# Keys and probabilities of a latent-attention branch turned by DMA instead of by TensorE

## What is computed

```python
q = (_rmsnorm(q_lat, q_norm_g) @ wq_b).reshape(b, s, MLA_HEADS, MLA_NOPE + MLA_ROPE)
kv = (_rmsnorm(kv_lat, kv_norm_g) @ wkv_b).reshape(b, s, MLA_HEADS, MLA_NOPE + MLA_V)
k_nope, v = kv[..., :MLA_NOPE], kv[..., MLA_NOPE:]
k = jnp.concatenate([k_nope, jnp.broadcast_to(k_pe[:, :, None, :], ...)], axis=-1)
q, k = _rmsnorm(q, qn_g), _rmsnorm(k, kn_g)          # then the last 64 columns are rotated
def attend(q_blk):
    sc = jnp.einsum('bhqd,bhkd->bhqk', q_blk, k).astype(jnp.float32) * scale
    p = jax.nn.softmax(sc, axis=-1)
    return jnp.einsum('bhqk,bhkd->bhqd', p, v)
return jax.nn.silu(gate) * o
```

## Time and profile before

| | |
|---|---|
| runs | 787.21, 787.49, 788.39 us (median 787.49) |
| profiled execution | 787.33 us, of which the trace spans 785.4 |
| TensorE matmuls | busy 779.3 us, 99% of the span |
| DVE / ACT / POOL | busy 558.1 / 417.6 / 65.5 us |
| DMA | 163 MB, 208 GB/s in the mean |
| granted TensorE clock | 1.0 in the mean |

### The profile page before, as it was taken

The page is one execution under the profiler, slowest core; times in us unless marked ns, Lnnn a source line. Parts: engine busy times, 40 slices in busy tenths (PEclk is TensorE's granted clock), DMA queues, the critical chain, the costliest instruction groups (busy, mean ns, idle before and its releaser), DMA issues.

```text
span 785.4 us, 9964 instructions
## 1 busy us (share of the span) xinstructions
PE 779.3 (99%) x3852; PEld 659.7 (84%) x3852; DVE 558.1 (71%) x698; ACT 417.6 (53%) x579; POOL 65.5 (8%) x46
## 2 busy tenths in 40 slices
PE   8999999999999999999999999999999999999998
PEld 7988888888887888888889888888888878888887
DVE  6864599778577756767896727986786597566684
ACT  7576765645344634533564676574545254454331
POOL 0122020100002100000000301100010021000000
PEclk9999999999999999999999999999999999999999
DMA  9796875587562837878766958675674647468785
GB/s 304 275 293 215 240 241 173 174 212 213 176 197 97 261 108 213 229 204 254 223 191 238 280 169 270 195 193 177 152 254 141 184 153 232 136 191 240 203 236 164
DMA packets 97086, 163.02 MB, mean 208 GB/s; under 512 B 57856, under 2 KB 60416, under 8 KB 96912
## 3 DMA queue, kind: packets, MB, share of 16 engines
q1 hardware_dynamic: 96432, 159.93, 67.8%
q10 hardware_dynamic: 432, 1.22, 0.5%
q0 software_dynamic: 176, 1.25, 0.4%
HBM read 147.17 MB, written 2.10 MB: 190 GB/s over the span
## 4 chain that ended last, share of the span: by engine, by line
PE 94%; DVE 3%; ACT 1%; DMA 1%; issue 0%; SPq 0%; ACTq 0%
PE pair L525 65%; PE bank L484 14%; PE pair L484 6%; PE bank L452 1%; PE bank L567 1%; PE bank L445 1%; PE bank L768 1%; PE bank L662 1%; DVE work L1480 1%; DVE lo L1097 1%; PE bank L758 1%; DMA raw<-stream 1%; DVE gate L1398 1%; PE bank L688 1%; PE bank L449 0%
## 5 line engine op out<-in xcount | busy, mean ns | idle before, releaser
L1097 DVE TENSOR_TENSOR lo<-raw,hi 128x1024 fp32r<-128x1024 f32 (+3 forms) x264 | 313.4, 1204 | 125.1 <-ACT hi L805 123.2
L805 ACT ACTIVATE hi<-raw 128x1024 fp32r<-128x1024 f32 (+3 forms) x264 | 264.9, 1021 | 226.0 <-PE pair L525 87.5
L525 PE MATMUL pair<-hi,xT_hi 128*128 128x512 f32 (+1 forms) x768 | 206.0, 388 | 0.7 <-ACT hi L874 0.6
L525 PE MATMUL pair<-lo,xT_hi 128*128 128x512 f32 (+1 forms) x768 | 202.9, 384 | 1.3 <-DVE lo L1097 1.2
L525 PE MATMUL pair<-hi,xT_lo 128*128 128x512 f32 (+1 forms) x768 | 202.8, 384 | 0.0
L525 PEld LDWEIGHTS pair<-lo,xT_hi 128*128 128x128 f32 x768 | 142.6, 188 | 30.3 <-DVE lo L1097 3.0
L525 PEld LDWEIGHTS pair<-hi,xT_lo 128*128 128x128 f32 x768 | 143.2, 188 | 28.1
L525 PEld LDWEIGHTS pair<-hi,xT_hi 128*128 128x128 f32 x768 | 140.7, 188 | 27.7 <-issue 1.1
L484 PE MATMUL bank<-hi,yT 128*128 128x512 f32 x320 | 79.0, 389 | 0.0
L484 PEld LDWEIGHTS bank<-hi,yT 128*128 128x128 f32 x320 | 60.1, 188 | 12.5
L484 PE MATMUL bank<-lo,yT 128*128 128x512 f32 x160 | 42.8, 389 | 0.0
(11 more groups left out here) (176 smaller groups left out, 664.6 us busy)
## 6 DMA issues: line engine op xcount, KB each, us to landing
raw<-stream SPq DMA_DIRECT2D x264, 512.0 KB, 4.3
raw<-stream SPq DMA_DIRECT2D x16, 256.0 KB, 5.1
xT<-x_in SPq DMA_DIRECT2D x16, 128.0 KB, 4.6
out<-xT SPq DMA_DIRECT2D x3, 512.0 KB, 6.7
consts<-consts_in POOLq DMA_DIRECT2D x1, 1152.0 KB, 8.3
mats<-mats_in ACTq DMA_DIRECT2D x2, 576.0 KB, 5.5
turned<-work SPq DMA_TRANSPOSE x34, 4.9
out<-xT SPq DMA_DIRECT2D x4, 128.0 KB, 1.7
```

The lines of the kernel that those rows point to most:

```text
L525: return nc.tensor.matmul(pair[a][m][:, 0:width], x_part[:, slots[i], m * P:(m + 1) * P], w_part[r][:, i * 512:i * 512 + width], start=(sl ...
L805: nc.scalar.activation(cut[0], cut[1], ACT.Copy).then_inc(rounded[r].sem, 1)
L1097: nc.vector.tensor_tensor(cut[0], cut[1], cut[2].bitcast(F32), ALU.subtract).then_inc(split[r].sem, 1)
```

## The change

- Keys (`k`) and probabilities (`p0` for the first 128 queries, `p1` for the others) go by DMA. TensorE's 8 turns of keys and 16 of probabilities per layer go, with the copies out of PSUM behind them.
- u is parted by ACT right behind its making, and its two DMAs stand ahead of granules 45 and 46. The DMAs of k stand ahead of 48 and 49, of p0 ahead of 57 and 58, of p1 ahead of 60 and 61; zb and D move two granules back.
- ACT parts u and k and joins k, D and B; DVE parts p0 and p1 and joins zq, u, p0, p1 and rq. POOL joins nothing.
- `times_v` runs per 128 queries, after granules 58 and 61. ACT's step on the second mixer's output moves from behind granule 83 to behind 85. The rotary key's arithmetic on DVE moves a few instructions back.

```diff
-TURNS = (("zq", 1), ("q", 2), ("u", 1), ("zb", 1), ("D", 1), ("rq", 1), ("B", 1), ("A", 1), ("C", 1),
+TURNS = (("zq", 1), ("q", 2), ("u", 1), ("k", 2), ("p0", 1), ("p1", 1), ("zb", 1), ("D", 1), ("rq", 1), ("B", 1), ("A", 1), ("C", 1),
...
+                if name in ("p0", "p1"):
+                    sp.dma_start_transpose(turned_tile[:, m], halves[:, m]).then_inc(turned.sem, 16)
...
-                    for name, at, parts in (("zq", 20, parts_q), ("q", 39, parts_h), ("u", 55, parts_h),
-                                            ("zb", 64, parts_h), ("D", 68, parts_y), ("rq", 85, parts_r),
+                    for name, at, parts in (("zq", 20, parts_q), ("q", 39, parts_h), ("u", 45, parts_h),
+                                            ("k", 48, parts_k), ("p0", 57, probs_parts[0]),
+                                            ("p1", 60, probs_parts[1]), ("zb", 66, parts_h), ("D", 70, parts_y), ("rq", 85, parts_r),
...
-                for f in range(2):
-                    pe.wait_ge(*la_ready.at(l, f + 1))
-                    pe.wait_ge(*k_scaled.at(l, 1))
-                    turn(2 + f, [kv_sb[:, m, h, 0:NOPE] for h in (2 * f, 2 * f + 1)
-                                 for m in range(MT)]).then_inc(tk_filled.sem, 1)
...
-                turn_probs(0)
-                turn_probs(1)
-                granules(56)
+                granules(59)
+                pe.wait_ge(*probs_ready.at(l, 8))
+                pe.wait_ge(*whole_ready.at(l, TURN["p0"]))
                 times_v(0)
+                granules(62)
+                pe.wait_ge(*whole_ready.at(l, TURN["p1"]))
                 times_v(1)
...
                 take("pv", lambda m: u[:, m, :], x_rs, u_ready)
+                nc.scalar.activation(parts_h, area(6400, 1024).bitcast(U16).rearrange("p (m c a) -> p m a c", m=MT, a=2),
+                                     ACT.Copy).then_inc(parted.sem, 1)
...
+                splits(46)
+                act.wait_ge(*k_scaled.at(l, 1))
+                for m in range(MT):
+                    nc.scalar.activation(parts_k[:, m].rearrange("p a (h c) -> p a h c", h=HEADS),
+                                         kv_sb[:, m, :, 0:NOPE].bitcast(U16).rearrange("p h (c a) -> p a h c", a=2),
+                                         ACT.Copy).then_inc(parted.sem, 1)
...
+                splits(51)
+                join(whole_k, "k")
...
-                splits(84)
+                splits(86)
                 act.wait_ge(*ob_filled.at(l, 1))
...
+                splits(20)
+                join(whole_q, "zq")
...
+                    if d:
+                        join(whole_u, "u")
                     dve.wait_ge(*la_ready.at(l, d + 1))
...
+                splits(56)
+                part_probs(0)
+                splits(57)
+                part_probs(1)
...
                 splits(59)
-                keep_probsT(2)
-                keep_probsT(3)
+                join(probsT[0].rearrange("p h j t -> p (h j t)"), "p0")
...
-                join(whole_u, "u")
-                pool.wait_ge(*k_b_ready.at(l, 2))
-                join(whole_d, "D")
```

More of the change, by code:

```diff
@@ L849, in round_whole, with join @@
                                              ).then_inc(rounded_.sem, 1)
+                def join(words, name):
+                    act.wait_ge(*turned.at(l, 32 * TURN[name]))
+                    nc.scalar.activation(words.bitcast(U16).rearrange("p (t a) -> p a t", a=2),
+                                         turned16[:].rearrange("p (a k) t -> p a (k t)", a=2), ACT.Copy
+                                         ).then_inc(whole_ready.sem, 1)
                 def round_tile(kt):
@@ L980, in _ @@
                                              ).then_inc(kr_rounded.sem, 1)
+                splits(51)
+                join(whole_k, "k")
+                act.wait_ge(*whole_ready.at(l, TURN["k"]))
+                nc.scalar.activation(yT_hi[:, SLOT["A"]:SLOT["A"] + HEADS, :],
+                                     whole_k.rearrange("p (h t) -> p h t", h=HEADS), ACT.Copy,
+                                     scale=gains[:, G_QK + 1:G_QK + 2]).then_inc(kT_rounded.sem, 1)
                 splits(55)
@@ L1054, in _ @@
                 splits(97)
+                join(whole_b, "B")
                 round_whole(whole_b, "B", yTB_rounded, SLOT["B"], G_Y + SLOT["B"])
@@ L1304, in _ @@
                     op0=ALU.mult, op1=ALU.subtract).then_inc(qT_ready.sem, 1)
-                def lo_pair(rounded_, ready, b0, slot0, gain):
-                    for f in range(2):
-                        dve.wait_ge(*rounded_.at(l, f + 1))
-                        at = slice(slot0 + 2 * f, slot0 + 2 * f + 2)
-                        nc.vector.scalar_tensor_tensor(
-                            out=yT_lo[:, at, :], in0=bank[b0 + f][:].rearrange("p (h t) -> p h t", h=2),
-                            scalar=gains[:, gain:gain + 1],
-                            in1=yT_hi[:, at, :].bitcast(F32),
-                            op0=ALU.mult, op1=ALU.subtract).then_inc(ready.sem, 1)
+                zpe = zlat[:, :, LAT_W - ROPE:LAT_W]
+                chained(nc.vector.tensor_tensor(kpe[:], zpe, rope_tab[:, 1, 0], ALU.mult))
+                for a in range(2):
+                    chained(nc.vector.tensor_tensor(kpe_x[:, :, a * half:(a + 1) * half],
+                                                    zpe[:, :, (1 - a) * half:(2 - a) * half],
+                                                    rope_tab[:, 1, 1, :, a * half:(a + 1) * half], ALU.mult))
+                chained(nc.vector.tensor_tensor(kpe[:], kpe[:], kpe_x[:], ALU.add))
                 splits(45)
@@ L1400, in gated @@
                             in1=y[:, m, at], op0=ALU.mult, op1=ALU.mult).then_inc(ready.sem, 1)
-                for m in range(MT):
-                    gated(m, gate0, m, p_inv, yD_ready)
+                splits(61)
+                dve.wait_ge(*gate0_ready.at(l, MT))
+                dve.wait_ge(*pv_done.at(l, 1))
+                gated(0, gate0, 0, p_inv, yD_ready)
+                splits(62)
+                join(probsT[1].rearrange("p h j t -> p (h j t)"), "p1")
+                splits(64)
+                dve.wait_ge(*pv_done.at(l, 2))
+                gated(1, gate0, 1, p_inv, yD_ready)
                 part(gate0_row, yD_ready, 8, parts_y)
@@ L1429, in _ @@
                 splits(68)
+                join(whole_z, "zb")
                 edge = const("edge").rearrange("p (e g t) -> p e g t", e=2, g=4)
@@ L1538, in _ @@
                 splits(89)
+                join(whole_r, "rq")
+                splits(90)
                 part(gate0_row, yB_ready, 8, parts_y)
```

136 lines of the change are left out of this document (49 added, 87 removed).

## The result

| | before | after |
|---|---|---|
| runs, median (us) | 787.49 (787.21 to 788.39) | 807.27 (806.36 to 807.54) |
| ratio, with its 95% interval | 1 | 1.0249 (1.0232 to 1.0266) |
| profiled execution / its span (us) | 787.33 / 785.4 | 806.36 / 804.5 |

Forecast were 799.0 us and 791.5 to 806.5. The direction and the places were right; the price was 19.8 us instead of 11.7.

A forecast was written before the change was run, and what follows sets the result against it. TensorE's matmuls, filling 99% of the span, were taken as the bound. Per layer, waits of 9.6 us less 2.5 removed and 1.2 at granules 85 to 87 gave +5.85; two layers, +11.7 on 787.3: 799.0 us, range 791.5 to 806.5.

The forecast's parts named there:

- another case: Rival: TensorE's clock falls to half rate in its waits, once per layer, giving 804.5 us; chance 12%.

The follow-up runs named there:

- the filled run: The changed kernel with 11 idle matmuls of 512 columns on TensorE between granule 50 and the wait of the scores; measured 804.25 us.

## What to carry to other kernels

A queue that waits for a chain of other engines' work delays every transfer listed behind it: ask of each new entry when its condition comes true, and put it behind the loads that are wanted before that time. Here moving one pair of entries by two gave back 16.6 of 19.8 us, and moving six places turned a loss of 2.5% into a gain of 1.0%. When a wait is removed, look for the stage it had covered, as waits hide one another; and price half clock behind a wait as part of the wait, not as another case, where TensorE is what comes last.

## What the runs showed of the hardware

- **Half clock behind short waits.** TensorE's clock fell behind waits of 2.80, 2.78 and 2.84 us in after, each time shortly after work had begun again. The wait of 2.65 at granule 48 of layer 1 was not followed by it, the same wait of the filled run, 2.63, was: the first four matmuls behind it took 1.15 us and 2.04 (TensorE, below). In the run with k at 50 a wait of 1.98 was followed by it, and one of 1.62 was not; with the scores one granule later one of 2.09 was; with p1 and u moved one of 2.11 was not, and with the keys back on TensorE one of 1.95 was not. The length of the wait alone doesn't tell. Layer 1 of after and then of the filled run, whose granted clock is 0.50 from 526.80 to 530.20:

```profile
526.60 1.15 PE L536 MATMUL pair<-hi,xT_hi 128*128 128x512 f32 x4 [2.65 <-ACT hi L792]
527.16 2.04 PE L537 MATMUL pair<-hi,xT_hi 128*128 128x512 f32 x4 [2.63 <-ACT hi L797]
```

- **Parts and joins differ on ScalarE.** The part of u (reads every second 16-bit word, writes in a row) took 1.91 us; joins of as many elements (read in a row, write every second word) took 2.51 to 2.56 in three buffers. On VectorE the two took 1.22 and 1.33. Whether the order of access is the cause or the buffers are was not tried. By the Trainium skill, "ScalarE: Activation LUTs", section "What ACT_TABLE_LOAD costs", both should take about 1.9 (an estimate from its rate and fixed part); the joins' rows differ, and hold here. The joins' means go from 2507 ns (below) to 2558:

```profile
L841 ACT ACTIVATE work<-turned 128x2048 uint16<-128x2048 uint16 x2 | 5.0, 2507 | 0.0
```
